# Opening of a two-layer decoder step: paired small loads, GpSimd squares, TensorE sums and a flat order on ScalarE and VectorE

## What is computed

```python
def _rms_norm(x, g):
    xf = x.astype(jnp.float32)
    y = xf * lax.rsqrt(jnp.mean(xf * xf, axis=-1, keepdims=True) + EPS) * g.astype(jnp.float32)
    return y.astype(x.dtype)

def _mem_kv(mem, g, w_kv, k_g):
    n = mem.shape[0]
    kv = _rms_norm(mem, g) @ w_kv
    mk = kv[..., :X_DIM].reshape(n, N_MEM, N_X_HEADS, HEAD_DIM)
    mv = kv[..., X_DIM:].reshape(n, N_MEM, N_X_HEADS, HEAD_DIM)
    return _rms_norm(mk, k_g), mv
...
for i in range(DEPTH):
    h = _rms_norm(x, p["norm_mix"][i])
    z = h @ p["w_in_att"][j]      # layer 0; then heads, attention, w_out, MLP
```

## Time and profile before

| | us |
|---|---|
| median of 3 runs (lowest, highest) | 1167.59 (1166.1, 1168.38) |
| the profiled execution | 1164.45 |
| its span | 1162.7 |
| TensorE matmul busy in the span | 1137.8 (98%) |
| VectorE, ScalarE, GpSimd busy | 804.2, 522.2, 130.7 |
| first matmul starts | 12.55 |
| attention panel 0, panel 1 start | 42.44, 49.84 |

### The profile page before, as it was taken

One profiled execution on the slowest core, in us unless ns is written; L12 is line 12 of the kernel. 1 busy time (PEld: TensorE's weight loads), 2 busy tenths in 40 slices (PEclk: granted clock), 3 DMA queues, 4 the chain that ended last, 5 costly groups with the idle time before them and its releaser, 6 DMA issues.

```text
span 1162.7 us, 22189 instructions
## 1 busy us (share of the span) xinstructions
PE 1137.8 (98%) x8998; PEld 1098.3 (94%) x8998; DVE 804.2 (69%) x1201; ACT 522.2 (45%) x902; POOL 130.7 (11%) x140
## 2 busy tenths in 40 slices
PE   5999999999999999999999999999999999999998
PEld 5899646999999999999999999999999999999998
DVE  6789975798577468558658545689856846756853
ACT  7623786366136227326433232446713722732630
POOL 0038752000000000000240131200000000000000
PEclk9999999999999999999999999999999999999999
DMA  8543141223313213312622321131331332231231
GB/s 336 189 160 119 51 166 52 73 74 109 109 37 122 103 67 108 108 64 81 216 73 73 146 87 64 71 110 61 122 108 39 111 108 72 96 121 44 101 137 48
DMA packets 23146, 120.18 MB, mean 103 GB/s; under 512 B 2708, under 2 KB 6932, under 8 KB 9892
## 3 DMA queue, kind: packets, MB, share of 16 engines
q1 hardware_dynamic: 17892, 100.93, 24.7%
q0 software_dynamic: 1632, 10.54, 2.5%
q10 hardware_dynamic: 3552, 7.74, 1.9%
HBM read 111.29 MB, written 5.69 MB: 101 GB/s over the span
## 4 chain that ended last, share of the span: by engine, by line
PE 94%; DVE 2%; ACT 2%; POOL 1%; DMA 0%; issue 0%; ACTq 0%; DVEq 0%; POOLq 0%
PE zps L505 53%; PE zps L779 25%; PE ops L779 4%; PE zps L767 4%; PE tps L649 1%; PE ops L677 1%; PE tps L534 1%; POOL sm L1900 1%; DVE w_lo L929 1%; PE zps L603 1%; ACT w_hi L1410 1%; ACT act_hi L1410 1%; DVE sm L1063 0%; PE zps L610 0%; PE tps L610 0%; DMA memx<-memT 0%
## 5 line engine op out<-in xcount | busy, mean ns | idle before, releaser
L505 PE MATMUL zps<-act_hi,w_hi 128*128 128x272 f32 x1664 | 348.6, 291 | 0.9 <-DVE w_lo L929 0.9
L505 PE MATMUL zps<-act_hi,w_lo 128*128 128x272 f32 x1664 | 344.0, 288 | 0.0
L505 PE MATMUL zps<-act_lo,w_hi 128*128 128x272 f32 x1664 | 343.2, 288 | 0.0
L779 PE MATMUL zps<-xf,wf 128*128 128x272 f32 x2304 | 298.7, 289 | 0.1
L779 PEld LDWEIGHTS zps<-xf,wf 128*128 128x128 f32 x2304 | 294.1, 188 | 0.7 <-issue 0.3
L505 PEld LDWEIGHTS zps<-act_hi,w_hi 128*128 128x128 f32 x1664 | 262.2, 188 | 5.4 <-issue 2.9
L505 PEld LDWEIGHTS zps<-act_lo,w_hi 128*128 128x128 f32 x1664 | 261.5, 188 | 0.0
L505 PEld LDWEIGHTS zps<-act_hi,w_lo 128*128 128x128 f32 x1664 | 260.0, 189 | 0.0
L1410 ACT ACTIVATE w_hi<-w_stage 128x2048 fp32r<-128x2048 f32 (+1 forms) x61 | 114.7, 1883 | 151.3 <-PE zps L505 123.9
L929 DVE TENSOR_TENSOR w_lo<-w_stage,w_hi 128x2048 fp32r<-128x2048 f32 x59 | 137.6, 2333 | 43.5 <-ACT w_hi L1410 43.2
L1410 ACT ACTIVATE wf<-w_sum 128x1024 fp32r<-128x1024 f32 x64 | 67.9, 1061 | 195.4 <-DVE w_sum L947 90.4
(11 more groups left out here) (184 smaller groups left out, 1270.4 us busy)
## 6 DMA issues: line engine op xcount, KB each, us to landing
w_stage<-wst SPq DMA_DIRECT2D x92, 1024.0 KB, 4.9
kx<-xkT POOLq DMA_DIRECT2D x4, 1024.0 KB, 8.6
vx<-xv POOLq DMA_DIRECT2D x4, 1024.0 KB, 7.0
x_res<-xT ACTq DMA_DIRECT2D x2, 1088.0 KB, 7.8
tmp<-z ACTq DMA_DIRECT2D x32, 68.0 KB, 2.1
yT<-x_res ACTq DMA_DIRECT2D x7, 272.0 KB, 2.1
memx<-memT SPq DMA_DIRECT2D x2, 512.0 KB, 4.6
vb<-swav POOLq DMA_DIRECT2D x1, 1024.0 KB, 9.9
```

Of the source, the lines that this page charges most:

```text
L505: mm = pe.matmul(zps[slot][:, h, 0:n], w_[:, d, k, w:w + 128], r_[:, k, c0 + h * n:c0 + (h + 1) * n], start=(j == 0 and i == 0), stop=(j = ...
L779: mm = pe.matmul(bank, wf_hl[pw][:, fw, a, :], x_form(l, px, fx, a)[:, 0, :], start=(begin and a == 0 and j == 0), stop=(a == KC // 2 - 1 ...
```

## The change

1. **Loads.** SyncE issues four pairs, each 256 KB of memory and 256 KB of the weights (0, 0), then (0, 1) whole. New semaphores `ld_mem0` to `3` and `ld_w0` to `2` mark them.
2. **Panels.** `first_panels` makes (0, 0) and (0, 1) side by side: for each pair of chunks, 6 products for one and 6 for the other. Panels with p >= 2 now use the second bank of their buffer.
3. **Squares of the memory** are made by GpSimd (8 operations), those of X by GpSimd's `sum_squares(2)` (15 operations) in place of ScalarE's 8 and VectorE's 7. `colsum(2)` waits for it.
4. **Memory's sums** are 16 products of TensorE, after both panels, in place of 2 products and VectorE's three folds.
5. **Order.** ScalarE and VectorE run one flat list; ScalarE loads its table at the start, by a square root over a zeroed tile; the loads of X are issued after the high parts of (0, 1); `turn_keys` moves; the cache loads of GpSimd move behind its sums.

```diff
+            for i in range(4):
+                c = slice(2 * i, 2 * i + 2)
+                sp.dma_start(memx[:, c, :], memT[:, c, :]).then_inc(ld[f"mem{i}"], 16)
+                sp.dma_start(stage[:, 0, c], wst[0, :, c]).then_inc(ld[f"w{i}"] if i < 3 else w_in[0], 16)
+            sp.dma_start(stage[:, 1], wst[1]).then_inc(w_in[1], 16)
...
-                elif n == 2:
-                    pe.wait_ge(x0_add, KC - 1)
                 else:
-                    pe.wait_ge(sq_acc, 1)
+                    pe.wait_ge(sq_acc, n // 2)
...
+            def first_panels():
+
+                for i in range(4):
+                    pe.wait_ge(m_los[0], 2 * i + 2)
+                    if i < 3:
+                        pe.wait_ge(w_los_part, i + 1)
+                    else:
+                        pe.wait_ge(w_los[0], 1)
+                    for p in range(2):
+                        for k in (2 * i, 2 * i + 1):
+                            memory_products(0, p, k)
...
             def memory_sums():
 
-                pe.wait_ge(m_sum, 3)
+                pe.wait_ge(one_rdy, 1)
+                pe.wait_ge(m_sq, KC)
                 for tb in range(2):
-                    mm = pe.matmul(tps[:, tb, 0:1], msq[:, 0, tb * 128:(tb + 1) * 128], ones[:, 0:1], start=True, stop=True)
+                    for k in range(KC):
+                        mm = pe.matmul(tps[:, tb, 0:1], msq[:, k, tb * 128:(tb + 1) * 128], one[:, :],
+                                       start=(k == 0), stop=(k == KC - 1))
...
+            first_panels()
+            memory_sums()
+            for l, p in ((0, 2), (0, 3), (1, 0), (1, 1), (1, 2)):
+                memory_panel(l, p)
             pe.wait_ge(ld["con2"], 16)
-            for l in range(2):
-                for p in range(4):
-                    memory_panel(l, p)
-                    if p == 3:
-                        turn_keys(2 * l)
-                    if (l, p) == (1, 0):
-                        turn_keys(1)
+            turn_keys(0)
+            turn_keys(1)
+            memory_panel(1, 3)
 
             for i in range(12):
                 panel(Q_ATT + i // 4, i % 4, *act_hl[0], ready=normed(0) if i == 0 else None)
                 if i == 0:
+                    turn_keys(2)
                     turn_keys(3)
                     colsum(2, NT)
...
-            pool.wait_ge(ld["x1"], 16)
-            pool.dma_start(vb[:, :, :], swav).then_inc(ld["vb"], 16)
+            pool.memset(tails[:, 0, :], 0.0).then_inc(zeroed, 1)
+            pool.memset(eps_t[:, :], EPS).then_inc(zeroed, 1)
+            pool.memset(one[:, :], 1.0).then_inc(one_rdy, 1)
+            for k in range(KC):
+                if k % 2 == 0:
+                    pool.wait_ge(ld[f"mem{k // 2}"], 16)
+                pool.tensor_tensor(msq[:, k, :], memx[:, k, :], memx[:, k, :], ALU.mult).then_inc(m_sq, 1)
+            sum_squares(2, X, NT, lambda k: pool.wait_ge(ld[("x", "x1")[k // 4]], 16))
```

More of the change, by code:

```diff
@@ L122, in build_kernel @@
     con, _ = place("con", [128, C_N])
+    one, _ = place("one", [128, 1])
+    eps_t, _ = place("eps_t", [128, 1])
     nsink, _ = place("nsink", [128, 16])
@@ L194, in build_kernel @@
         headones = con[:, C_HEAD:C_HEAD + 128]
[L195 removed]
+        eps = eps_t[:, 0:1]
         def gain(norm, k):
@@ L554, in memory_panel @@
                         pe.wait_ge(m_los[l], k + 1)
[L555 to L558, removed]
+                    memory_products(l, p, k)
             def memory_sums():
-                pe.wait_ge(m_sum, 3)
+                pe.wait_ge(one_rdy, 1)
@@ L1291, in _ @@
             dve.wait_ge(ld["con"], 16)
-            dve.wait_ge(ld["mem0"], 16)
-            for k in range(KC):
[L1294 to L1306, removed]
+            for i in range(4):
+                c = slice(2 * i, 2 * i + 2)
+                dve.wait_ge(ld[f"mem{i}"], 16)
+                for k in (2 * i, 2 * i + 1):
+                    memory_lo(0, k)
+                if i < 3:
+                    dve.wait_ge(w_his_part, i + 1)
+                else:
+                    dve.wait_ge(w_his[0], 1)
+                dve.tensor_tensor(w_lo[:, 0, c], stage[:, 0, c], w_hi[:, 0, c].bitcast(f32), ALU.subtract).then_inc(
+                    w_los_part if i < 3 else w_los[0], 1)
@@ new lines, in split_lo_halves @@
+            def split_lo_halves(q, d):
+                for half, made, n, done in ((0, w_his_half, q + 1, w_los_half), (1, w_his[d], q + 1, w_los[d])):
+                    c = slice(half * 4, half * 4 + 4)
+                    dve.wait_ge(made, n)
+                    dve.tensor_tensor(w_lo[:, d, c], stage[:, d, c], w_hi[:, d, c].bitcast(f32), ALU.subtract).then_inc(done, 1)
+            split_lo_halves(0, 1)
+            link(dve.tensor_scalar(nsink[:, :], con[:, C_SINK:C_SINK + 16], -1.0, None, ALU.mult))
@@ L1326, in _ @@
-            dve.wait_ge(ld["rope"], 16)
+            split_lo_halves(1, 0)
+            for m in range(2):
+                key_sums(m)
+            split_lo(1, 1)
+            for m in range(2):
+                key_norm(m)
+            for k in range(4):
+                norm_lo(0, k, 0)
+            split_lo(2, 0)
+            for m in (2, 3):
+                key_sums(m)
+            for k in range(4, KC):
+                norm_lo(0, k, 0)
+            for m in (2, 3):
+                key_norm(m)
@@ new lines, in _ @@
+            square_key(0, 1)
+            split_hi(1, 1)
+            root_keys(0)
+            root_keys(1)
+            take_memory(0, 2)
+            take_memory(0, 3)
+            act.wait_ge(ld["x"], 16)
+            for k in range(4):
+                norm_hi(0, k, 0)
+            take_memory(1, 0)
+            square_key(1, 0)
+            split_hi(2, 0)
+            take_memory(1, 1)
+            square_key(1, 1)
+            act.wait_ge(ld["x1"], 16)
+            for k in range(4, KC):
+                norm_hi(0, k, 0)
@@ L1793, in _ @@
+            keys_out(0)
+            keys_out(1)
+            root_keys(2)
+            root_keys(3)
+            take_memory(1, 2)
+            take_memory(1, 3)
+            split_hi(2, 1)
             for i in range(12):
@@ L1798, in _ @@
                 if i == 0:
+                    act.dma_start(cs[:, :, :], rope).then_inc(ld["rope"], 16)
                     root_tokens(2, NT)
```

146 lines of the change are left out of this document (54 added, 92 removed).

## The result

The changed kernel takes 1173.55 us in the median of 13 runs (1170.97 to 1179.05), the kernel before 1166.11 beside it (13 runs): ratio 1.0060, 95% interval 1.0048 to 1.0072, 7 us slower. The time forecast was 1172.3, from 1167.6. The profiled execution took 1175.19, which is 10.7 above the profiled one of before; its span is 1172.9, 10.2 above. The two medians differ by 7.4 only: the profiled execution of before was among its fastest, that of the changed kernel above its median.

The account below looks back on a forecast made before the run. TensorE, busy 98% of the span, bounds the kernel, so the start of attention panel 1 counts: 3.8 us later plus 0.9 for the clock, 4.7 in sum, 1167.6 to 1172.3; its own range 1170.0 to 1174.6, 8 in 10 1163.6 to 1174.8.

Parts of the forecast that it names:

- its step of 4.7: Whole kernel: 3.8 us later start of attention panel 1 plus 0.9 for the clock, added to the median.
- The start: Opening: smaller first loads bring TensorE's first product to 7.3 us, 5.2 earlier than before.
- The other pairs come 1.3 apart: Opening loads: pairs after the first arrive every 1.3 us against TensorE's 2.6 per pair, so nothing starves it.
- Memory's sums: Opening, TensorE: 16 products in place of 2, 32 rows at 0.11 us, 3.5 against 0.7.
- The transfers: Opening loads: X requested at 12.0, second part landed at 21; weights (1, 0) behind it, landed at 23.7.
- The forecast's wait of 2.0: TensorE ahead of panel (1, 0): wants its weights at 24.3, low half made at 26.3; waits 2.0, then 0.9.
- GpSimd beside VectorE: Opening: the two take turns, 19.6 us of GpSimd work; (2, 0) made at 44.7, panel 1 3.8 us later.
- The first rival: Opening: GpSimd doesn't hold VectorE up; panel 1 at 46.4, 3.4 us faster, 1164.2; chance 0.26.
- The second: Opening: VectorE always goes first; panel 0 at 40.7, panel 1 at 52.7, 2.9 us slower, 1170.5; chance 0.12.
- The clock: TensorE ahead of panel 0: standing still 7.1 us may lower its clock; 0.9 us taken, between 0 and 2.0.
- Nothing behind panel 1 changes: After attention panel 1 starts: the later requests of cache loads and rope table still precede their users.

Follow-up runs that it names:

- e1: The changed kernel with GpSimd's sum of X's squares cut to one of its 15 operations: 1167.0 us, ratio 1.0012 to the kernel before.
- e4: The kernel before with X's squares and their sum made by GpSimd in place of ScalarE and VectorE, nothing else: 1175.22 us, ratio 1.0073.
- e2: The changed kernel with ScalarE freeing panel 0's buffer ahead of the roots of the keys: 1171.47 us, ratio 1.0036 to the kernel before.
- e12: The kernel before with one wait more, panel 0 waiting for X's last addition: 1170.32 us, ratio 1.0033.
- e3: The changed kernel with X's squares back on ScalarE and their additions on VectorE, GpSimd keeping the memory's: 1170.17 us, ratio 1.0041 to the kernel before.
- e5: The changed kernel with both parts of X requested when the first pair has landed: 1176.54 us, ratio 1.0102 to the kernel before (4 runs).
- e10: The changed kernel with no GpSimd work in the opening, memory's sums folded by VectorE, X's first part requested early: 1169.13 us, ratio 1.0033 to the kernel before.
- e11: Run e10 with X's first part requested with the fourth pair and GpSimd's cache loads later: 1164.92 us, ratio 0.9992 to the kernel before.
- e7: Run e3 with X requested early as in e5 and the memory's squares on ScalarE too: 1170.68 us, ratio 1.0042 to the kernel before.
- e9: The changed kernel with memory's 16 one-column products spread over panel (0, 2) instead of one block: 1173.52 us, ratio 1.0056 to the kernel before.
- e13: Run e3 with the memory's squares on ScalarE too, X still requested late: 1169.68 us, ratio 1.0033 to the kernel before.
- e14: Run e11 with X's second part and the constants' rest requested when X's first part has landed: 1164.93 us, ratio 0.9990 to the kernel before.

## Why the prediction was right, and where it was off

The change is slower by the mechanism forecast: turns of GpSimd and VectorE (e1, e4), a wait of TensorE for panel 0's buffer behind VectorE (e2), and a clock that falls in it (e12). That the time forecast lies only 1.2 under the measured one is in part luck: it started from a median of 3 runs that was 1.5 above the later one of 13, and its step of 4.7 was 2.7 short in the opening alone. The terms:

- *The start.* Forecast 7.3 for the first product, measured 7.91; 4.6 earlier than before, not 5.2. "The other pairs come 1.3 apart" was wrong for the third, which ScalarE takes up at 9.4, 3.4 behind the second. Just before that little was transferred. The last number of these stretches is GB/s, of the changed kernel, then of the kernel before with its larger transfers:

```profile
6.00:7.50 1.50, 0.00 (x0) 0.00 (x0) 1.50 (x2) 1.50 (x4) 1.21 (x2) 1.00 0.80 157
```

```profile
6.00:7.50 1.50, 0.00 (x0) 0.00 (x0) 0.49 (x2) 1.49 (x4) 0.00 (x0) 1.00 1.01 426
```

  What made the dip isn't shown. TensorE, at the low clock until 11.1, waited only 0.45 for it.
- *Memory's sums.* Forecast 3.5, measured 4.7. The 0.11 a row was right at the high level (3.5 in e2 and e3); that the clock falls inside them, at 18.0, and stays low until 24.7 stood nowhere. It costs 1.2 in the sums and 1.9 in the 20 products behind them (0.21 for 0.12). Little of it counted, since weights (1, 0) were late as forecast: the first half was wanted at 24.3 and low at 26.3 (measured 26.6), and TensorE came later still, near 28. The forecast's wait of 2.0 was filled by the low clock, and (1, 3) ended at 40.0, where 39.0 was forecast.
- *The transfers.* (1, 0) landed at 24.0 for 23.7. X was requested at 13.9, not 12.0, and its second part landed near 29, not 21, beside the weights. The forecast took the queues as one line; e5, e10 and e11 show that they share. It mattered for weights (1, 1) at 29.1, a step that the forecast didn't list: VectorE waited 1.8 for them here, and 4.5 without GpSimd's turns (e3).
- *GpSimd beside VectorE.* 15 operations took 25.0 us from 19.0 to 44.0, as forecast (42.5 for the end). The low part of (2, 0) was made at 46.1 for 44.7, panel 0 started at 47.6 for 46.1. The sum left the two key norms out of the turns, though it names the keys' product as of this kind: they took 1.39 and 1.11, where they take 0.43 in e1. The first rival (no hold-up) asked for (2, 0) before 39; e1 shows that this is the kernel without GpSimd's sum. The second (VectorE always first) asked for panel 0 at 40.7 and for GpSimd's end behind 50; measured 47.6 and 44.0. The Trainium skill ("SBUF — State Buffer", "Who interferes with whom") calls the shared ports an exclusive lock and says that issue order decides who blocks; the pair at 31.09 and 31.11 agrees, 3.50 against 2.29. The pair of the last section, by its starts, doesn't.
- *The clock.* "I take 0.9, with 0 and 2.0 as ends": it was 2.1 (9.63 from panel 0's start to panel 1's, for 7.5 without it; granted clock 0.50 from 47.6 to 52.0). The undersized term; e12 measures it alone. The Trainium skill ("TensorE: Matmul & The Clock Gate", Part 1) says that an idle array goes back to the low level, and this wait agrees. By it the forecast's whole 2.0 was due and its sum 5.8; measured 7.4.
- *"Nothing behind panel 1 changes"* failed: in the profiled execution 2.8 us went there.

In the opening 7.4 against 4.7: 1.5 of the difference at panel 0's start, 1.2 at the clock.

## What to carry to other kernels

Before work is moved to GpSimd because VectorE is full, count VectorE's operations with two inputs in SBUF in that stretch: the two take turns, so the moved work is added to VectorE's list (e4: 4.9 us taken off, panel 0 8.7 later). Ask of every new wait of TensorE what the clock adds to it, and of every request that moves earlier with whose landing it shares and what its issuing engine has to put off for it (e5, e7). A gain ahead of a wait is worth nothing until that wait's own engine gets shorter.

## What the runs showed of the hardware

**Where the clock falls.** In the eight runs in which TensorE had waited 3.1 to 7.7 us ahead of panel 0 (changed, e2, e3, e7, e9, e10, e12, e13) the panel took 7.6 to 9.0; in the six with a wait of 1.8 or less (before, e1, e4, e5, e11, e14) 6.3. The longest wait didn't cost most: 7.6 behind 7.7 us (e9), 8.8 behind 3.5 (e7). Yet e14, which had waited 2.0 for (0, 1) until 17.0, ran the stretch 18 to 22 at a mean of 0.57. The clock also fell in all seven runs with the block of 32 one-column rows (changed, e1, e2, e3, e5, e7, e13), though TensorE was busy all through it: inside the block at 18.0 in the changed kernel, just behind it at about 20.9 in e2 and e3. It didn't where the rows were spread (e9).

**A later stage can lose by the phase of two engines.** In attention, VectorE's `head_norm_out` (L1016) starts at 127.80 here and GpSimd's first product of the rotation 0.02 later; at this place before, VectorE was done at 120.1 when GpSimd started at 120.48. VectorE of before, then of the changed kernel:

```profile
119.33 0.78 DVE L997 SCALAR_TENSOR_TENSOR z<-z,con,tmp 128x544 f32<-128x544 f32 x1
```

```profile
127.80 1.95 DVE L1016 SCALAR_TENSOR_TENSOR z<-z,con,tmp 128x544 f32<-128x544 f32 x1
...
127.82 1.35 POOL L1956 TENSOR_TENSOR z<-z,cs 128x544 f32<-128x544 f32 x1
```

1.95 in place of 0.78, while GpSimd kept its 1.35: a start 0.02 earlier in the profile didn't keep VectorE's time, unlike at 31.09. Why isn't shown. The transposes of v (L600) then waited 2.2 where they waited 0.5 before, and the clock stood at 0.50 in 139 to 143 us. Of the 14 profiled executions of this study the eight with a wait of 2.2 there (changed, e2, e5, e7, e9, e10, e11, e14) lost 2.0 to 7.4 us between panel 1 and the end against before's, seven of them with a fall of the clock in that stage; of the six with a wait of 0.9 or less none lost over 0.3. Each is a single execution, and no run changes this place alone, so that the phase is the cause is argued from the order of the rows, not shown. e14 belongs to the eight, which would be why its shorter opening didn't pay in full. What sets the phase wasn't tried.
